# Seven-product groups of a down projection: another order of their operands, and the first of four weight sums made by an accumulating transfer from GpSimd's queue

## What is computed

```
def swiglu(x, w_gate, w_up, w_down):
    return (jax.nn.silu(x @ w_gate) * (x @ w_up)) @ w_down

f = swiglu(rmsnorm(h, g_ffn1_pre[i]), w_ffn1_gate[i], w_ffn1_up[i], w_ffn1_down[i])
h = h + 0.5 * rmsnorm(f, g_ffn1_post[i])
```

## Time and profile before

| | us |
|---|---|
| median of 3 runs | 1903.43 (1902.51 to 1903.64) |
| the profiled execution | 1907.09 |
| its span in the trace | 1905.3 |
| PE busy | 1868.6 |
| DVE busy | 1253.8 |
| ACT busy | 938.5 |
| POOL busy | 112.9 |
| HBM read | 358.01 MB, 189 GB/s over the span |

### The profile page before, as it was taken

How to read it: one execution, slowest core, us unless ns; L and a number is a source line. 1 busy time by engine, 2 the same in 40 slices (tenths; PEclk the granted TensorE clock), 3 DMA queues, 4 the chain that set the end, 5 groups by cost and what they waited for, 6 DMA issues and landing times.

```text
span 1905.3 us, 24370 instructions
## 1 busy us (share of the span) xinstructions
PE 1868.6 (98%) x8562; PEld 1528.3 (80%) x8562; DVE 1253.8 (66%) x1400; ACT 938.5 (49%) x1239; POOL 112.9 (6%) x162
## 2 busy tenths in 40 slices
PE   9999999999999999999999999999999999999998
PEld 7888888888777778888888888888888887777886
DVE  5555554555797778787896755555554579867775
ACT  6444443444455446555565644444443455445563
POOL 1000000000000000012651100000000000000010
PEclk9999999999999999999999999999999999999999
DMA  8666666666555555655556566666666655655654
GB/s 258 206 201 206 194 191 204 217 214 211 198 191 198 159 185 183 201 168 165 157 180 200 165 212 207 203 205 201 200 192 198 221 200 185 209 187 183 213 189 144
DMA packets 214116, 371.55 MB, mean 195 GB/s; under 512 B 16592, under 2 KB 41632, under 8 KB 213664
## 3 DMA queue, kind: packets, MB, share of 16 engines
q1 hardware_dynamic: 213040, 367.20, 61.1%
q10 hardware_dynamic: 1008, 3.46, 0.5%
HBM read 358.01 MB, written 2.10 MB: 189 GB/s over the span
## 4 chain that ended last, share of the span: by engine, by line
PE 81%; DVE 12%; DMA 5%; ACT 1%; SPq 0%; issue 0%; DVEq 0%; POOLq 0%; POOL 0%; ACTq 0%
PE bank L654 26%; PE bank L656 25%; PE bank L655 25%; DVE w_rest L1539 7%; DMA raw<-in_w_ffn_down 5%; DVE branch L1551 1%; DVE branch L1547 1%; DVE branch L1549 1%; DVE branch L1546 1%; ACT w_high L1154 1%; PE bank L993 1%; PE bank L1022 1%; PE bank L1004 1%; PE bank L760 1%; DMA resid<-in_x 0%; PE bank L968 0%
## 5 line engine op out<-in xcount | busy, mean ns | idle before, releaser
L1525 DVE TENSOR_TENSOR w_rest<-raw,w_high 128x1024 fp32r<-128x1024 f32 x486 | 596.8, 1231 | 467.3 <-ACT w_high L1136 464.3
L1136 ACT CAST w_high<-raw 128x1024 fp32r<-128x1024 f32 x486 | 509.6, 1051 | 637.0 <-PE bank L656 493.2
L654 PE MATMUL bank<-w_high,x_high 128*128 128x512 f32 (+1 forms) x1912 | 745.7, 390 | 0.7 <-DVE x_rest L1966 0.2
L656 PE MATMUL bank<-w_high,x_rest 128*128 128x512 f32 (+1 forms) x1912 | 741.0, 388 | 0.0
L655 PE MATMUL bank<-w_rest,x_high 128*128 128x512 f32 (+1 forms) x1912 | 740.6, 387 | 0.0
L654 PEld LDWEIGHTS bank<-w_high,x_high 128*128 128x128 f32 x1912 | 359.1, 188 | 74.6 <-issue 1.6
L656 PEld LDWEIGHTS bank<-w_high,x_rest 128*128 128x128 f32 x1912 | 359.0, 188 | 73.8
L655 PEld LDWEIGHTS bank<-w_rest,x_high 128*128 128x128 f32 x1912 | 359.2, 188 | 71.6
L1539 DVE TENSOR_TENSOR w_rest<-raw,w_high 128x1024 fp32r<-128x1024 f32 x136 | 164.6, 1222 | 78.8 <-ACT w_high L1154 78.4
L1154 ACT CAST w_high<-raw 128x1024 fp32r<-128x1024 f32 x136 | 140.5, 1049 | 114.1 <-DMA raw<-in_w_ffn_down 58.3
L654 PE MATMUL bank<-w_high,h_high 128*128 128x512 f32 x448 | 176.3, 394 | 7.5 <-DVE w_rest L1539 7.5
(11 more groups left out here) (209 smaller groups left out, 1277.0 us busy)
## 6 DMA issues: line engine op xcount, KB each, us to landing
raw<-in_w_ffn_up SPq DMA_DIRECT2D x176, 512.0 KB, 4.6
raw<-in_w_ffn_gate SPq DMA_DIRECT2D x174, 512.0 KB, 4.4
raw<-in_w_ffn_down SPq DMA_DIRECT2D x144, 512.0 KB, 4.8
raw<-in_w_qkv SPq DMA_DIRECT2D x68, 512.0 KB, 4.0
branch<-in_w_ffn_down SPq DMA_DIRECT2D x32, 512.0 KB, 6.7
raw<-in_w_o SPq DMA_DIRECT2D x32, 512.0 KB, 4.2
raw<-in_w_ple_gate SPq DMA_DIRECT2D x32, 512.0 KB, 4.2
branch<-branch SPq DMA_DIRECT2D x320, 32.0 KB, 1.9
```

The lines of the kernel that those rows point to most:

```text
L654: nc.tensor.matmul(o[:, 0:width], xh, wh, start=first and c == 0, stop=False, skip_group_check=go_on)
L656: ins = nc.tensor.matmul(o[:, 0:width], xr, wh, start=False, stop=last and c == chunks - 1, skip_group_check=go_on)
L1136: nc.scalar.copy(slot(n, k)[0], raw[:, k]).then_inc(w_high_done, 1)
L1525: nc.vector.tensor_tensor(to_rest, raw[:, k], to_high.bitcast(F32), ALU.subtract).then_inc(w_rest_done, 1)
```

## The change

The order within a group becomes b11, sum1, b22, sum3, sum2, b21, sum4, with four plain operations threaded in, and the four groups of a pair stand back to back: 11 operations each (plain, b11, plain, plain, sum1, b22, sum3, sum2, b21, plain, sum4). Five plain operations stand ahead of them, seven behind.

sum1 is made no longer by DVE. POOL waits for b11's rest and issues a transfer that reads b12 from HBM and adds it onto b11 in SBUF; ACT's cast of sum1 waits for its landing. So b12 is read twice. DVE makes the other three sums directly after the rest of b22 (sum3, sum2) and of b21 (sum4). The two chain places are swapped from group to group, so that b11 of the next group can be loaded once sum3's rest is done; the first group of a stage uses `gain_row` as a place for b11. SP's chain loads are no longer tied to b22; each stands in the queue where its place is free (`CHAIN_AT`). The gain loads of the first pair move behind the first group. `combine` for the next group comes five operations ahead of its b11, its cast one step later. The accumulation of the odd bank and `fix_odd` end at another plain operation (`ODD_STOP`).

```diff
     def group(i, inner):
 
-        return ([(kind, None, i) for kind in ("b22", "b21", "b11", "sum1", "sum3", "sum2")] + inner
-                + [("sum4", None, i)])
+        own = [(kind, None, i) for kind in ("b11", "sum1", "b22", "sum3", "sum2", "b21", "sum4")]
+        return inner[0:1] + own[0:1] + inner[1:3] + own[1:6] + inner[3:4] + own[6:]
...
-    PAIR_ORDER = (plains(0, G0, G0 + 6) + group(0, plains(0, G0 + 6, G0 + 7)) + plains(0, G0 + 7, G0 + 10)
-                  + group(1, plains(1, G0, G0 + 1)) + plains(1, G0 + 1, G0 + 4)
-                  + group(2, plains(1, G0 + 4, G0 + 5)) + plains(1, G0 + 5, G0 + 8)
-                  + group(3, plains(0, G0 + 10, G0 + 11)) + plains(0, G0 + 11, FS) + plains(1, G0 + 8, FS))
+    PAIR_ORDER = (plains(0, G0, G0 + 5) + group(0, plains(0, G0 + 5, G0 + 9)) + group(1, plains(1, G0, G0 + 4))
+                  + group(2, plains(0, G0 + 9, G0 + 11) + plains(1, G0 + 4, G0 + 6))
+                  + group(3, plains(1, G0 + 6, G0 + 10)) + plains(0, G0 + 11, FS) + plains(1, G0 + 10, FS))
...
+    CHAIN_AT = [[RING_OPS[RING]] * 2] + [[after_op(PLACE[end, None, i - 1]) for end in ("sum3", "sum4")] for i in range(1, GROUPS)]
+    FIRST_OF = [["row", 1, 0, 1], [0, 1, 0, 1]]
+    SECOND_OF = [[1, 0, 1, 0], [1, 0, 1, 0]]
+    COMBINE_AT = [0] + [at - 5 for at in GROUP_AT[1:]]
...
+            def first_sums(n0, w, f):
+                for j in range(NBD // 2):
+                    for i in range(GROUPS):
+
+                        pool.wait_ge(w_rest_done, n0 + PAIR_OPS * j + GROUP_AT[i] + 1)
+                        pool.dma_start(chain(j, FIRST_OF[j][i]),
+                                       rows(w)[:, 2 * CPS * i:2 * CPS * i + CPS, (2 * j + 1) * NB:(2 * j + 2) * NB],
+                                       accum_op=ALU.add).then_inc(first_sum_landed, 16)
+
+            factors(factors_up_to(J_IN1))
+            first_sums(S_DOWN1, w_ffn1_down, 0)
             factors(factors_up_to(J_POST1))
...
+                elif kind == "sum1":
+                    act.wait_ge(first_sum_landed, 16 * (groups + i + 1))
+                    src = chain(j, FIRST_OF[j][i])
...
-                if kind == "b11":
-                    dve.wait_ge(chain_landed[1], 16 * (groups + i + 1))
-                    nc.vector.tensor_tensor(turns, turns, b12, ALU.add).then_inc(sum_ready, 1)
-                    nc.vector.tensor_tensor(b12, b12, b22, ALU.add).then_inc(sum_ready, 1)
-                elif kind == "sum1":
-                    nc.vector.tensor_tensor(turns, turns, b22, ALU.add).then_inc(sum_ready, 1)
-                else:
-                    nc.vector.tensor_tensor(turns, turns, b21, ALU.add).then_inc(sum_ready, 1)
+                if kind in ("b22", "b21"):
+                    turns, other = chain(j, FIRST_OF[j][i]), chain(j, SECOND_OF[j][i])
+                    if kind == "b22":
+                        dve.wait_ge(chain_landed[1], 16 * (groups + i + 1))
+                        nc.vector.tensor_tensor(other, other, src, ALU.add).then_inc(sum_ready, 1)
+                        nc.vector.tensor_tensor(turns, turns, src, ALU.add).then_inc(sum_ready, 1)
+                    else:
+                        nc.vector.tensor_tensor(turns, turns, src, ALU.add).then_inc(sum_ready, 1)
```

More of the change, by code:

```diff
@@ L86, in layer_program, with after_op @@
     PAIR_RING = RING_AT[PAIR_OPS]
+    RING_OPS = [t for t in range(PAIR_OPS) if PAIR_ORDER[t][0] in RING_KINDS]
     PLACE = {item: t for t, item in enumerate(PAIR_ORDER)}
-    GROUP_AT = [PLACE["b22", None, i] for i in range(GROUPS)]
+    GROUP_AT = [PLACE["b11", None, i] for i in range(GROUPS)]
     GROUP_END = [PLACE["sum4", None, i] for i in range(GROUPS)]
-    SUM_AT = {"sum1": 1, "sum3": 2, "sum2": 3, "sum4": 4}
-    COMBINE_AT = [0] + [at - 7 for at in GROUP_AT[1:]]
+    SUMS = 3
+    SUM_AT = {"sum3": 1, "sum2": 2, "sum4": 3}
+    def after_op(t):
+        return min(u for r, u in enumerate(RING_OPS) if r >= RING and RING_OPS[r - RING] >= t)
+    CHAIN_AT = [[RING_OPS[RING]] * 2] + [[after_op(PLACE[end, None, i - 1]) for end in ("sum3", "sum4")] for i in range(1, GROUPS)]
+    FIRST_OF = [["row", 1, 0, 1], [0, 1, 0, 1]]
+    SECOND_OF = [[1, 0, 1, 0], [1, 0, 1, 0]]
+    COMBINE_AT = [0] + [at - 5 for at in GROUP_AT[1:]]
     T_FIX, T_EVEN, T_ODD = GROUP_END[-1], GROUP_END[-1] + 3, PAIR_OPS - 1
+    ODD_STOP = G0 + 9
     assert PAIR_OPS % RING == 0 and PAIR_RING % RING == 0 and PAIR_ORDER[T_EVEN] == ("plain", 0, FS - 1)
+    assert PLACE["b22", None, GROUPS - 1] < PLACE["plain", 1, ODD_STOP] < T_FIX
     LAG = (PAIR_OPS - PAIR_RING) * (NBD // 2)
@@ L134, in layer_program @@
     U_PLE = U_P + 1
-    T_TURN_P = PLACE["plain", 1, FS - 5]
+    T_TURN_P = PLACE["plain", 1, FS - 4]
     UW = NB // BPB
@@ L465, in free_place, with chain_load @@
                                 else:
-                                    sums = 4 * (GROUPS * (2 * f + j0) + i)
+                                    sums = SUMS * (GROUPS * (2 * f + j0) + i)
                                     sp.wait_ge(sum_ready, sums + SUM_AT["sum2" if kind == "b22" else "sum4"])
+                def chain_load(j, i, b):
+                    if i == 0 and j == 0:
+                        if b:
+                            sp.wait_ge(turned, u_h + BPB)
+                    elif i == 0:
+                        sp.wait_ge(fixed_even, 2 * f + 1)
+                    elif i == 1 and j == 0 and b == 1:
+                        sp.wait_ge(turned, u_h + BPB)
+                    else:
+                        end = "sum4" if b else "sum3"
+                        sp.wait_ge(w_rest_done, n0 + PAIR_OPS * j + PLACE[end, None, i - 1] + 1)
+                    to = chain(j, (SECOND_OF if b else FIRST_OF)[j][i])
+                    sp.dma_start(to, part(2 * i, 2 * j + b)).then_inc(chain_landed[b], 16)
+                chain_load(0, 0, 0)
                 for j in range(NBD // 2):
-                    if j == 0:
-                        gain_load(0)
-                        gain_load(1)
                     for t, (kind, which, i) in enumerate(PAIR_ORDER):
+                        for g in range(GROUPS):
+                            for b in range(2):
+                                if t == CHAIN_AT[g][b] and (j, g, b) != (0, 0, 0):
+                                    chain_load(j, g, b)
                         if kind in RING_KINDS:
@@ L479, in down @@
                             sp.dma_start(raw[:, k], src).then_inc(w_landed[k], 16)
[L480 to L486, removed]
-                                else:
-                                    sp.wait_ge(turned, u_h + BPB)
-                                sp.dma_start(chain(j, b), part(2 * i, 2 * j + b)).then_inc(chain_landed[b], 16)
+                        if j == 0 and t == CHAIN_AT[1][1]:
+                            gain_load(0)
+                            gain_load(1)
                         if j and t == GROUP_END[0]:
@@ L919, in down @@
                                                i == G0 and not (which and tile == 0),
-                                               i == FS - 1 or (which == 1 and tile == 1 and i == G0 + 7),
-                                               go_on=which == 1 and i >= G0 + 8)
+                                               i == FS - 1 or (which == 1 and i == ODD_STOP),
+                                               go_on=which == 1 and i > ODD_STOP)
                             ins.then_inc(w_used, 1)
                         else:
-                            if j == 0:
+                            if j == 0 and kind in MIXED_AT:
                                 pe.wait_ge(comb_rest, GROUPS * f + i + 1)
-                            group_product(n, kind, i, target[kind],
-                                          i == 0 and target[kind] is not even[0] and target[kind] is not even[1],
-                                          i == GROUPS - 1 and target[kind] is not even[0] and target[kind] is not even[1])
+                            own = kind in ("b11", "sum1", "sum2", "sum3")
+                            group_product(n, kind, i, target[kind], i == 0 and (own or kind == "b22"),
+                                          i == GROUPS - 1 and own)
                         if j == 0 and t == 0:
@@ L1536, in rest_down @@
                 else:
-                    src = b12 if kind == "sum3" else turns
+                    src = chain(j, (SECOND_OF if kind == "sum3" else FIRST_OF)[j][i])
                 dve.wait_ge(w_high_done, n + 1)
@@ L1540, in rest_down @@
                                         ).then_inc(w_rest_done, 1)
-                if kind == "plain" or kind in ("b22", "b21", "sum3", "sum4"):
-                    return
-                b22, b21 = (raw[:, ring_item(j, PLACE[name, None, i])[1]] for name in ("b22", "b21"))
-                if kind == "b11":
-                    dve.wait_ge(chain_landed[1], 16 * (groups + i + 1))
```

(10 more changed lines are left out.)

26 lines of the change are left out of this document (16 added, 10 removed).

## The result

The changed kernel takes 1932.48 us (median of 4, 1932.21 to 1936.43) against 1902.97 (1902.31 to 1903.64) on the same chip: a ratio of 1.016, 95% interval 1.0142 to 1.0177. It is 29.5 us **slower**, where 16 us faster were forecast, and lies above the forecast's range.

The account below looks back on a forecast made before the run. PE's waits for w_rest in four pairs, 38.5 us, bound the gain; less 21.8 us lost to the new landing, 16.7 us are won: 1907.1 becomes 1890.4, less 3.7 gives 1887 us for the median, range 1866 to 1924.

Parts of the forecast that it names:

- What bounds the kernel: PE's waits for DVE's w_rest in the down stages' four pairs: 38.5 us, the most the change can win.
- The round: DVE's time between b11's rests: 17.7 + D in first pairs, 14.8 + D in second, against PE's 20.4 us.
- D: Time from b11's rest to the release of ACT's cast of sum1 by POOL's landing: taken as 6.1 us.
- the formulas: Lag of PE at a pair's last group: 4D - 14.6 us in first pairs, 4D - 23.3 in second, per stage.
- the slow rival: At ACT's cast of sum1: double reading and turns with SP's queue make D 8.2, 17 us slower, 1920; chance 0.19.
- The start: First group of a stage: SP's moved loads cost nothing; b11's rest stands at -1.7 us against PE's operation 5.
- The last subtraction: From profiled execution to median: 3.7 us taken off 1890.4, giving 1887.
- The rest: Raw-tile waits of 5.31 us don't return; DVE saves 18 us; the 0.93 us stop after combine goes.
- Adding at the cost of a copy: POOL's transfer lands like a plain load: D 5.2 gives 1877 us, D 3.7 gives 1865; chance 0.22.
- POOL held off while DVE works: POOL writes descriptors only once DVE pauses: D 9.5 and 7.2, 19 us slower, 1923; chance 0.05.

Follow-up runs that it names:

- the best version: Changed kernel, but DVE makes sum1 again and the first group's b12 load stands four raw loads back in SP's queue: 1874.24 us.
- one experiment: Changed kernel, but POOL's transfer copies b12 over b11 instead of adding it: 1896.9 us.
- another: Changed kernel, but POOL's transfer adds only the first of the two chunks of b12, 256 KB instead of 512 KB: 1894.72 us.
- The kernel without the stop at the start: Changed kernel, but the first group's b12 load, which waits for the transposes, is issued four raw loads later in SP's queue: 1919.09 us.
- the kernel with b11 first: Changed kernel, but b11 stands ahead of the group's first plain operation, so three plain operations lie between b11 and sum1: 1928.84 us.

## Why the prediction was wrong

**What bounds the kernel: right.** The 38.5 us of lost time in the four pairs as the most that can be won held: the best version wins 30.1 against the median, outside the windows the kernel after changed by 0.4 us, and within them PE waits for nothing but DVE's w_rest.

**The round: right.** 17.7 + D in the first pair gives 26.4, 25.9 and 25.8 for the D read off the trace (8.7, 8.2, 8.1); the distances of L1588 are 26.4, 25.95 and 25.8. In the second pair 14.8 + D gives 23.2 and 24.5 for 8.4 and 9.7, measured 23.2 and 24.6. Only the first round of a second pair is 0.9 to 1.0 longer than the formula (22.3 for a D of 7.5, measured 23.2 in the first stage); there ACT still waits for PE between the operations, so that the round is not all in series on DVE. The slope, 16 us per us of D, stood in one experiment (35.6 for 2.3) and roughly in another (37.8 for 2.8, where 41 follow with the second pairs at their floor).

**D: mis-sized, and this decided the sign.** The step that failed is "the nearest rows are those of 1024 KB on a queue that isn't SP's ... I take the middle one, D = 5.9 + 0.2 = 6.1". Read as above for all sixteen, from 6.3 to 9.7, D is 8.1 on average. With 8.1 the formulas give 1919, so this term alone turns the forecast gain into a loss. Two things were not in those rows. POOL's instruction takes 1.20 us of the time to landing, where an issue of SP takes 0.37 (that no byte moves before it ends is not shown; the copy, with 0.5 us less of it, fits). And an adding transfer has 3.4 us of every engine, as the slow rival had it (twice 1.5). Three rows of transfers of double size from another queue were likeness, not measurement, and the middle of three was given nearly half of the chances although each us was worth 16.

The rival "the landing holds the round", at D = 8.2 and 1920, is what happened, with the start on top; its chance of 0.19 was too small. That its 8.2 meets the 8.1 is partly luck: it let turns with SP's queue double the engine time, to 6 us. Between the copy and the adding transfer the engine time differs by 1.7 us and the landing, less the issue, by 1.8; no doubling shows. What is left of the landings, 7.8 and 5.5, less issue and engine time, is 3.2 and 3.1, where the rival had 2.0.

**The start: a term left out.** "SP issues the same loads, each where its place comes free" was wrong for the first group. Its load of b12 waits for the transposes of the hidden values, and in the new place in the queue raw loads stand behind it that could have gone out. b11's first rest ended at 506.46 while PE was due at its operation 5 at 503.96: +2.5, not the -1.7 carried over from the earlier trace rows. That is 4.2 per first pair, 8.4 in all.

**The last subtraction.** The formulas give the loss whole: PE's own time and what is lost make 1907.1 - 38.5 + 21.8 = 1890.4 for any execution of the new kernel. The 3.7 us by which the profiled execution of before stood above its median were then taken off once more, to 1887. The kernel after has no such excess (profiled 1932.56, median 1932.48), and outside the windows its profiled execution is as long as the one of before, to 0.4 us.

**The sum.** 2.0 us more of D at 16 are 32, and the start's 8.4 make 40; the lost time came out at 63.7 against the 21.8 forecast, 42 more. With the 3.7 it is 44 of the 45.5 us between 1887 and 1932.48. The kernel without the stop at the start is a second test: with its own D of 7.8 the formulas give 48.4 us lost, and its span of 1915.7, 10.4 above 1905.3, shows 48.9. (That its median of 1919.09 equals the 1919 above is a coincidence.)

**The rest: mostly right.** The raw tiles' 5 us waits inside the groups are gone. DVE's saved 18 us were of no use once DVE idles for the landing. No stop after combine shows in the first pairs' rounds, which 17.7 + D meets to 0.1 us.

**The other rivals.** Adding at the cost of a copy: refuted by the queue's row, 2.8% against 1.4%. POOL held off while DVE works: POOL's 14 issues onto branch take 1.203 us at the least and 1.207 at the most, in the first pair behind b11's rest, where DVE works without a gap, as in the second, where it does not; each starts 0.4 us after the rest. The two onto gain_row take 1.38 and 1.28. No holding shows, which agrees with what the Trainium skill, "SBUF — State Buffer", section "Who interferes with whom", says of tensor_tensor and descriptors. By the fit of the Trainium skill, "DMA: Bandwidth & Descriptors", section "Anatomy of one DMA", such a transfer was estimated at 3.2 us. Here a copy from POOL's queue landed after 5.5 (4.1 at the least) and an adding one after 7.8. The measurement decides: beside the other traffic of these stages, some 200 GB/s in all, the fit is far too short.

## What to carry to other kernels

Price an instruction that is to leave an engine by what replaces it in the dependency round, not by the busy time it saves: 1.14 us of DVE were traded for 8 us of landing in a chain that DVE itself goes round. Where a trace has no row for the new operation and the slope is steep, the unknown is the forecast; its range of signs should weigh more than the middle of its likest rows. When loads of one queue are moved, look at what each waits for and how many stand behind it, at the first turn too and not only in the steady state.

## What the runs showed of the hardware

An adding transfer of 512 KB from HBM onto SBUF took twice the engine time of a copy of the same bytes from the same queue (3.4 and 1.66 us per engine), with 4352 packets against 2304 for the sixteen. GpSimd's instruction for it took 1.20 us, for the copy 0.72 to 0.74, for half the bytes added 0.86 to 0.88; the first of each stage took 0.1 to 0.2 us more.

TensorE's granted clock fell around its longest stops: in the window

```profile
540.00:550.00 10.00, 7.54 (x26) 5.88 (x27) 9.20 (x9) 5.71 (x6) 0.00 (x0) 0.83 0.29 103
```

it is 0.83 on average, a mixture of the two levels of 1.2 and 2.4 GHz, around PE's wait of 3.39 us that ends at 542.17; the first matmul behind it is recorded with 0.77 us. The first pairs' means are 0.98 and 0.96. In the kernel with b11 first PE stopped as long in all in its first stage (22.1 us of waits for w_rest, 20.6 in the kernel after), but for 1.8 us at the longest, and its clock was 0.999 over the span. The formulas, with each group's own D and without a term for the clock, explain the four windows to 1 us each, so it cost little here: PE had to wait for DVE in any case.
